# The cross-partition sum of squares of five norms as two float32r products, with three of them four blocks later

## What is computed

```python
def rmsnorm(x, g):
    xf = x.astype(jnp.float32)
    y = xf * lax.rsqrt(jnp.mean(xf * xf, axis=-1, keepdims=True) + RMS_EPS)
    return (y * g.astype(jnp.float32)).astype(x.dtype)

def swiglu(x, w_gate, w_up, w_down):
    return (jax.nn.silu(x @ w_gate) * (x @ w_up)) @ w_down
...
        x = x + out
        x = x + swiglu(rmsnorm(x, norm_ffn[l]), f_wg[l], f_wu[l], f_wd[l])
```

## Time and profile before

| | |
|---|---|
| median of 3 runs | 1759.73 us (1759.6 to 1761.24) |
| the profiled execution's own time | 1759.4 us |
| its span, first to last instruction | 1757.4 us |
| busy: TensorE / VectorE / ScalarE / GpSimd | 1742.7 / 1075.4 / 723.5 / 289.6 us |
| granted TensorE clock, mean | 0.999 |

### The profile page before, as it was taken

The page is one execution under the profiler, slowest core; times in us unless marked ns, Lnnn a source line. Parts: engine busy times, 40 slices in busy tenths (PEclk is TensorE's granted clock), DMA queues, the critical chain, the costliest instruction groups (busy, mean ns, idle before and its releaser), DMA issues.

```text
span 1757.4 us, 28222 instructions
## 1 busy us (share of the span) xinstructions
PE 1742.7 (99%) x9986; PEld 1707.8 (97%) x9986; DVE 1075.4 (61%) x1895; ACT 723.5 (41%) x1186; POOL 289.6 (16%) x415
## 2 busy tenths in 40 slices
PE   9999999999999999999999999999999999999998
PEld 8979999999999999999999999999999889999998
DVE  8987755544579755554476655555458877555533
ACT  6465333333378433333222333333334574333332
POOL 4354100001215400001100210000132444000011
PEclk9999999999999999999999999999999999999999
DMA  8322333333333433333433333333446113433341
GB/s 307 105 73 75 117 120 120 121 129 132 114 114 112 136 128 120 121 116 133 135 117 130 112 127 123 120 120 120 132 139 224 62 61 109 140 121 119 132 136 68
DMA packets 63990, 216.98 MB, mean 123 GB/s; under 512 B 7168, under 2 KB 9040, under 8 KB 63664
## 3 DMA queue, kind: packets, MB, share of 16 engines
q1 hardware_dynamic: 59664, 202.34, 34.8%
q0 software_dynamic: 3280, 12.12, 2.3%
q10 hardware_dynamic: 976, 1.61, 0.2%
HBM read 212.38 MB, written 3.66 MB: 123 GB/s over the span
## 4 chain that ended last, share of the span: by engine, by line
PE 91%; DVE 4%; ACT 2%; issue 1%; POOL 0%; DMA 0%; SPq 0%; DVEq 0%; POOLq 0%; ACTq 0%
PE bank L810 28%; PE bank L809 27%; PE bank L808 27%; PE bank L992 1%; DVE w_lo L1491 1%; PE bank L973 1%; PE bank L975 1%; PE bank L974 1%; PE bank L1039 1%; PE bank L1018 1%; ACT w_hi L1163 1%; PE bank L998 1%; PE bank L1045 0%; DVE cv L1866 0%; DMA x<-in_x_t 0%
## 5 line engine op out<-in xcount | busy, mean ns | idle before, releaser
L1491 DVE TENSOR_TENSOR w_lo<-raw,w_hi 128x1024 fp32r<-128x1024 f32 x381 | 488.3, 1286 | 297.1 <-ACT w_hi L1163 295.4
L808 PE MATMUL bank<-a_hi,w_hi 128*128 128x400 f32 (+2 forms) x1936 | 667.2, 345 | 1.9 <-DVE w_lo L1491 1.3
L809 PE MATMUL bank<-a_lo,w_hi 128*128 128x400 f32 (+2 forms) x1936 | 665.5, 344 | 0.0
L810 PE MATMUL bank<-a_hi,w_lo 128*128 128x400 f32 (+2 forms) x1936 | 664.9, 343 | 0.0
L1163 ACT ACTIVATE w_hi<-raw 128x1024 fp32r<-128x1024 f32 x381 | 398.9, 1052 | 330.4 <-PE bank L810 326.7
L808 PEld LDWEIGHTS bank<-a_hi,w_hi 128*128 128x128 f32 (+1 forms) x1936 | 362.4, 187 | 5.9 <-issue 2.1
L810 PEld LDWEIGHTS bank<-a_hi,w_lo 128*128 128x128 f32 (+1 forms) x1936 | 364.8, 188 | 0.7
L809 PEld LDWEIGHTS bank<-a_lo,w_hi 128*128 128x128 f32 (+1 forms) x1936 | 362.7, 187 | 1.5
L810 PE MATMUL bank<-h_hi,w_lo 128*128 128x400 f32 (+1 forms) x704 | 240.8, 342 | 0.0
L809 PE MATMUL bank<-h_lo,w_hi 128*128 128x400 f32 (+1 forms) x704 | 240.1, 341 | 0.0
L808 PE MATMUL bank<-h_hi,w_hi 128*128 128x400 f32 (+1 forms) x704 | 239.2, 340 | 0.0
(11 more groups left out here) (283 smaller groups left out, 1782.6 us busy)
## 6 DMA issues: line engine op xcount, KB each, us to landing
raw<-in_w_all SPq DMA_DIRECT2D x382, 512.0 KB, 3.5
bias_p<-rel_scratch POOLq DMA_DIRECT2D x2, 2176.0 KB, 11.8
k_s<-in_ck_t POOLq DMA_DIRECT2D x4, 512.0 KB, 8.0
v_c<-in_cv POOLq DMA_DIRECT2D x2, 1024.0 KB, 16.5
ki_s<-in_cki_t POOLq DMA_DIRECT2D x4, 256.0 KB, 5.9
x<-in_x_t SPq DMA_DIRECT2D x2, 400.0 KB, 6.0
out_v_t<-v_f POOLq DMA_DIRECT2D x2, 400.0 KB, 5.3
out_y_t<-yg SPq DMA_DIRECT2D x2, 384.0 KB, 2.6
```

The costliest lines, as they stand in the source:

```text
L808: pe.matmul(out, wh, hi[:, kc, c0:T], start=(first and n == 0), stop=False)
L809: pe.matmul(out, wh, lo[:, kc, c0:T], start=False, stop=False)
L810: mm = pe.matmul(out, wl, hi[:, kc, c0:T], start=False, stop=(last and n == len(blocks) - 1))
L1491: nc.vector.tensor_tensor(w_lo[:, s, :], raw[:, s, :], w_hi[:, s, :].bitcast(F32), ALU.subtract).then_inc(lo_ready, 1)
```

## The change

Five norms (1, 3, 4, 5, 7) no longer sum `sqsum` with one float32 product. ScalarE writes its rounded part `sq_hi`, VectorE the remainder `sq_lo`, and TensorE multiplies both by a float32r matrix of ones into the same sum. In norms 1, 3 and 7 the pair is issued behind block 0 of unit 2, 17 blocks into the stage; in norms 4 and 5 it stays behind block 4 of unit 1. `sq_hi` lies in the memory of `std`, `sq_lo` in that of `sq`.

```diff
+SPLIT_NORMS = (1, 3, 4, 5, 7)
...
+        sq_hi, sq_lo = at("sq_hi", [128, T], F32R, rsq + 8 * T), at("sq_lo", [128, T], F32R, rsq)
+        ones_r = sb("ones_r", [128, 128], F32R)
...
                 else:
                     pe.wait_ge(acc_ready, acc_count(n + 1, 0))
+                if n in SPLIT_NORMS:
+                    pe.wait_ge(squares_lo, SPLIT_NORMS.index(n) + 1)
+                    pe.matmul(bank[4][:, 0:T], ones_r[:], sq_hi[:], start=True, stop=False)
+                    pe.matmul(bank[4][:, 0:T], ones_r[:], sq_lo[:], start=False, stop=True).then_inc(ss_done, 1)
+                    return
                 pe.matmul(bank[4][:, 0:T], ones[:], sqsum[:], start=True, stop=True).then_inc(ss_done, 1)
...
-                             after=lambda n, j=j: sum_squares(norm) if j == 1 and n == 4 else None)
+                             after=lambda n, j=j: sum_squares(norm) if (j, n) == ((1, 4) if norm in (4, 5) else (2, 0)) else None)
...
             def rms(n):
                 if n == 0:
                     act.wait_ge(pool_set, 2)
+                if n in SPLIT_NORMS:
+                    if n == SPLIT_NORMS[0]:
+                        nc.scalar.activation(ones_r[:], ones[:], ACT.Copy)
+                    act.wait_ge(acc_ready, acc_count(n + 1, 0))
+                    nc.scalar.activation(sq_hi[:], sqsum[:], ACT.Copy).then_inc(squares_hi, 1)
                 act.wait_ge(ss_done, n + 1)
...
             def rms(n):
+                if n in SPLIT_NORMS:
+                    dve.wait_ge(squares_hi, SPLIT_NORMS.index(n) + 1)
+                    nc.vector.tensor_tensor(sq_lo[:], sqsum[:], sq_hi[:].bitcast(F32), ALU.subtract).then_inc(squares_lo, 1)
                 dve.wait_ge(std_ready, n + 1)
```

More of the change, by code:

```diff
@@ L398, in program @@
         in_bias = sem("in_bias")
+        squares_hi, squares_lo = sem("squares_hi"), sem("squares_lo")
         zeroed, ZEROED = sem("zeroed"), 5 + NL
```

## The result

| | before | changed |
|---|---|---|
| median, 19 runs each | 1759.68 us (1759.36 to 1761.64) | 1763.27 us (1762.5 to 1764.9) |
| profiled execution: time, span | 1759.4, 1757.4 us | 1763.85, 1762.0 us |

The ratio is 1.002, with a 95% interval from 1.0014 to 1.0027: 3.6 us slower, where +3.2 and 1762.9 us were forecast.

The account below looks back on a forecast made before the run. TensorE, busy 1742.7 of 1757.4 us, was taken as the bound. Norm terms 1.92 + 1.01 + 0.89 - 0.31 - 0.31 gave +3.2 us on 1759.4, or 1762.6; with 0.3 for the median, 1762.9 us, range 1761.0 to 1764.9.

Parts of the forecast that it names:

- Two float32r products for one float32: TensorE, each of five norms: 0.365 us for two products replaces 0.675, so 0.31 us less per norm.
- The bound of 0.34 a product: Upper bound on each new product's time, half the float32 sum, at which nothing is gained; 0.182 was forecast.
- The chain of 5.69 us behind the sum: Sum, root, reciprocal, unit 3's split: its line-809 product comes no earlier than 5.69 us after the sum's start.
- Norm 3, +1.01: Sum moved to 598.22; unit 3's late split puts its line-809 product at 603.91 instead of 602.90.
- Norm 7, +0.89: Sum at 1477.15, no wait for `sqsum`; unit 3's line-809 product at 1482.84 instead of 1481.95.
- Norm 1, +1.92: TensorE waits 1.7 us for `sq_lo` behind `softplus()`, then for unit 3's split; product at 191.91, not 189.99.
- Norms 4 and 5, -0.31 each: Place kept; sum, root, reciprocal and split all come 0.31 us earlier, with no new wait.
- The sum, +3.2: Total over five norms: 1.92 + 1.01 + 0.89 - 0.31 - 0.31 = +3.2 us.
- the cheap case: Rival: unit 3's splits are in time after all; -1.55 to -1.9 us, 1758.0 us; 6%.
- the case of half the loss: Only the wait in norm 1 costs time, +1.2 to +2 us; 6%.
- The dear products: Rival: new products cost 0.34 us each like the float32 halves; +4.75 us, 1764.5 us, slower; 5%.
- The lost clock: Rival: TensorE drops to 1.2 GHz in norm 1; +4.4 us for one unit, 1767.3 us in all; 5%.

Follow-up runs that it names:

- the later place alone: Kernel before with its float32 sums, only the sum's place in norms 1, 3 and 7 moved four blocks later: +3.00 us inner stretch, +2.75 median.
- norms 4 and 5 alone: Kernel before with only the sums of norms 4 and 5 split, at their old place: -0.67 us inner stretch, -1.02 median, ratio 0.9985 to 1.0003.
- five split sums, the old place: Changed kernel with all five split sums behind block 4 of unit 1: +6.50 us inner stretch, +5.33 median against the kernel before.
- With norm 1 left, the old place: Norms 3, 4, 5, 7 split, all behind block 4 of unit 1; norm 1 keeps its float32 sum: +0.97 us inner stretch, +1.10 median against kernel before.
- The early split: Changed kernel with unit 3's split ahead of root and reciprocal on ScalarE and VectorE: -0.40 us inner stretch, -0.48 median against the kernel before.
- the best version: Changed kernel, unit 3's split ahead of root and reciprocal, `softplus()` spread behind four gate products: -2.74 us inner stretch, median 1757.01 us, ratio 0.9974 to 0.9992.
- the version with norm 1 left: Changed kernel, unit 3's split ahead of root and reciprocal, norm 1 keeping its float32 sum at the old place: -2.39 us inner stretch, -2.65 median.

## Why the prediction was right

Step by step, in the changed kernel's trace:

- *Two float32r products for one float32*, 0.31 us saved: measured 0.73 against 1.04 from product to product, and -0.67 us for two norms alone. The bound of 0.34 a product did not come into it.
- *The chain of 5.69 us behind the sum*: 601.55 to 607.24 in norm 3, exactly, and in norm 7 from 1480.86 to 1486.55.
- *Norm 3, +1.01*: the sum stood 3.33 us later than its forecast place (601.55, 598.22) and the product 4.34 later than before (607.24, 602.90), so +1.01. *Norm 7, +0.89*: the sum stood 3.71 later than its forecast place (1480.86, 1477.15), the product 4.60 later than before (1486.55, 1481.95), so +0.89.
- *Norm 1, +1.92*: +2.0, with the waits at 1.67 and 1.09.
- *Norms 4 and 5, -0.31 each*: the displacement (how much later than in the kernel before the sum starts) fell from 4.34 at norm 4's sum (889.10 against 884.76) to 4.02 at norm 5's (1029.40 against 1025.38) and 3.71 at norm 7's, this one counted from its forecast place.
- *The sum, +3.2*: +3.27 in the stretch, +3.59 by the medians.

Of the rivals, the cheap case is out. The profile shows the three late splits, and the later place alone costs 3.0 us with none of the new products. With these waits in norms 3 and 7, the case of half the loss (a wait in norm 1 alone) is out too. The dear products are out by the norms 4 and 5 alone. The lost clock did not occur in the traced execution of the changed kernel: the clock stayed full through a wait of 1.67 us, 4 us of work and one of 1.09. The other executions were not traced; their times lie within 2.4 us, those of the kernel before within 2.3, so a loss of 4.4 us in some of them is not to be seen. That no row of the kernel before could say so made this step a bet and not a reading. It was the right thing to fear: with the wait at 3.83 us the clock fell, and 2.6 us went with it in that execution. The time lies on the border of what was called slower (3.5 us, a ratio of 1.0020, in the middle of the interval), so on which side of it the median fell is chance, as the 42% and 55% said.

The prediction priced the later place only against the kernel before, where the sum is a float32 product. The experiments add what it is worth once the sum is split. With five split sums, the old place is worse still (+6.50 against +3.27 in the stretch), and all of that is norm 1, with its long wait and the half clock behind it. With norm 1 left, the old place is the better one by 0.3 us (+0.97 against +1.28). The fault of the later place is that unit 3's split stands behind the reciprocal, and `sq_lo` behind `softplus()`; with both mended the products' gain arrives.

It does not arrive alone, though. Of the 2.7 us that the best version gains, the products' share is 5 x 0.31 = 1.55. The rest is time that the kernel before lost already: 0.95 at the split in norm 1, as the version with norm 1 left shows, and some 0.25 from norm 7, whose sum no longer waits for `sqsum` (0.14 us for the wait and 0.11 for the wake-up, by the forecast's rows). The early split without any split sum was not run; by these numbers most of that 1.2 us is to be had without the new products.

## What to carry to other kernels

When one engine is the bound and the others run in written order, cost an edit by the chain from the moved instruction to the next thing that the bound engine waits for, not by the work that it adds or removes. Here an edit that saves 1.5 us of products came out at +3.6 us as it was first made, at -0.5 with a 1.2 us split put ahead of a reciprocal, and at -2.8 with `softplus()` out of the way too. Before an instruction is put later, look at what is queued behind its consumer on every engine that takes part, and move that first.

## What the runs showed of the hardware

- **Behind a single wait of 3.83 us TensorE's granted clock was at 0.50, 1.2 GHz instead of 2.4, in the middle of the kernel**, and it was full again at 192.2 us, 5.8 us after work had resumed. In the traces here, waits of 1.67 and 1.09 us with 4 us of work between, and single ones of 1.24, left it full. The Trainium skill ("TensorE: Matmul & The Clock Gate", What's actually happening) says that idleness puts the clock at a half and sustained work at the full; the trace agrees (0.50 from 186 to 192 us, then full).
- **Shorter waits can do it too, in some executions and not in others.** Within `attention(0)`, ahead of everything edited here, TensorE waits twice, with 1.1 us of work between. In the last-named run at the old place with norm 1 left, its timeline and the windows of all engines (the clock again behind the POOL column) show:

```profile
113.19 0.51 PE L1002 MATMUL bank<-kz,q_t 128*128 128x144 f32 x2 [0.58 <-DVE nmx L1797]
115.37 0.33 PE L1028 MATMUL bank<-cst,lg 128*128 128x128 f32 x1 [1.13 <-issue]
```

```profile
112.00:116.00 4.00, 2.29 (x16) 1.53 (x16) 3.81 (x16) 2.82 (x11) 1.13 (x4) 0.94 0.43 123
116.00:120.00 4.00, 4.00 (x29) 2.65 (x25) 1.50 (x8) 2.02 (x9) 2.05 (x5) 0.63 0.04 12
```

  The kernel before has the same two waits, 0.58 and 1.12 us, and kept its full clock there in the profiled execution. So the length of a wait alone does not say whether the clock falls, and no safe length can be read from these runs. The fall costs some 1.5 us here: from the second wait's product to the next product of line 985 behind it (975 before) there are 3.76 us (115.37 to 119.13) where the kernel before has 2.21 (115.00 to 117.21). Of the ten traces of this case, three show this fall: the later place alone, norms 4 and 5 alone, and this run.
- The times of most versions fall into two groups some 1.8 us apart (1759.5 and 1761.3 for the kernel before), and the three traced executions with this fall are all in the upper one. That the fall makes the groups is likely, and not shown. It is not the only thing that differs ahead of norm 1: the changed kernel's traced execution has its full clock there and is 1.3 us late all the same.
